# Two fused transformer blocks on one core: a 512-wide input product in the second block, a shorter inverse root, a one-step last stage, and a new interleaving

## The reference

```python
h = rmsnorm_2(x, g_pre) * (1.0 + scale[:, None, :]) + shift[:, None, :]
proj = jnp.einsum('bsd,de->bse', h, w_in)                # 1024 -> 3584
gu, gv, gg, rq, rk, rv, rg = jnp.split(proj, PROJ_SPLITS, axis=-1)   # 7 x 512
y_gmlp = gmlp_branch(gu, gv, gg, gmlp_ln_g, gmlp_ws, gmlp_bs)        # 4 groups of 128
y_ret = retention_branch(rq, rk, rv, rg, positions, ret_gn_g)        # 4 heads of 128
y = jnp.concatenate([y_gmlp, y_ret], axis=-1)
y = rmsnorm_2(jnp.einsum('bsm,md->bsd', y, w_out), g_post)
return x + gate[:, None, :] * y
```

## Time and profile before

| | |
|---|---|
| median of three executions | 3868.55 us |
| the profiled execution, its own time | 3869.71 us |
| its span, first to last instruction | 3867.9 us |
| TensorE busy | 3667.3 us, 95% |
| VectorE, ScalarE, GpSimd busy | 1910.7, 1698.8, 800.3 us |
| mean granted TensorE clock | 0.983 |
| TensorE idle in the waits listed, summed | 192.7 us |

### The profile page before, as it was taken

The page is one execution under the profiler, slowest core; times in us unless marked ns, Lnnn a source line. Parts: engine busy times, 40 slices in busy tenths (PEclk is TensorE's granted clock), DMA queues, the critical chain, the costliest instruction groups (busy, mean ns, idle before and its releaser), DMA issues.

```text
span 3867.9 us, 55010 instructions
## 1 busy us (share of the span) xinstructions
PE 3667.3 (95%) x21288; PEld 3203.9 (83%) x21288; DVE 1910.7 (49%) x4115; ACT 1698.8 (44%) x3455; POOL 800.3 (21%) x704
## 2 busy tenths in 40 slices
PE   7999889999998999999999999999999999999998
PEld 6888777888778888888878988888879987888897
DVE  4346563545656664546545555344567753111443
ACT  4334544555655444535544444343556543111322
POOL 3443333444454332110011100011000000000100
PEclk9999899999999999999999999999999999999999
DMA  6887557677676567455454556445453455545454
GB/s 167 270 252 208 176 166 254 217 254 267 238 251 223 182 228 275 162 192 177 158 187 145 170 193 218 166 170 188 155 201 132 145 191 209 195 175 199 170 185 145
DMA packets 327701, 760.01 MB, mean 196 GB/s; under 512 B 52625, under 2 KB 212369, under 8 KB 271122
## 3 DMA queue, kind: packets, MB, share of 16 engines
q1 hardware_dynamic: 266386, 720.83, 53.7%
q10 hardware_dynamic: 61056, 35.67, 3.5%
HBM read 581.00 MB, written 175.39 MB: 196 GB/s over the span
## 4 chain that ended last, share of the span: by engine, by line
PE 75%; DVE 12%; ACT 6%; issue 3%; ACTq 2%; POOL 1%; DMA 1%; SPq 0%; DVEq 0%
PE PS L1375 21%; PE PS L1377 21%; PE PS L1376 21%; PE PS L1493 2%; PE PS L1483 2%; PE PS L1474 2%; PE PS L1475 2%; PE PS L1507 1%; DVE PP L2093 1%; POOL WF L2322 1%; ACTq L1716 1%; PE PS L1453 1%; DVE BIG L1947 1%; ACT WF L1613 1%; DVE PT L2050 1%
## 5 line engine op out<-in xcount | busy, mean ns | idle before, releaser
L1375 PE MATMUL PS<-WF,BIG 128*128 128x256 f32 (+1 forms) x2328 | 726.7, 312 | 17.4 <-POOL WF L2322 6.5
L1377 PE MATMUL PS<-WF,BIG 128*128 128x256 f32 (+1 forms) x2328 | 712.4, 306 | 0.0
L1376 PE MATMUL PS<-WF,BIG 128*128 128x256 f32 (+1 forms) x2328 | 712.3, 306 | 0.0
L1375 PE MATMUL PS<-BIG,WF 128*128 128x512 f32 (+1 forms) x1792 | 687.1, 383 | 12.9 <-DVE BIG L1947 8.0
L1377 PE MATMUL PS<-BIG,WF 128*128 128x512 f32 (+1 forms) x1792 | 676.7, 378 | 0.0
L1376 PE MATMUL PS<-BIG,WF 128*128 128x512 f32 (+1 forms) x1792 | 676.3, 377 | 0.0
L2322 POOL TENSOR_TENSOR WF<-RAW,WF 128x512 fp32r<-128x512 f32 x380 | 507.0, 1358 | 746.7 <-ACT WF L1613 746.5
L1375 PEld LDWEIGHTS PS<-WF,BIG 128*128 128x128 f32 x2328 | 450.5, 194 | 44.1 <-issue 6.6
L1376 PEld LDWEIGHTS PS<-WF,BIG 128*128 128x128 f32 x2328 | 451.0, 194 | 21.3 <-issue 2.4
L1377 PEld LDWEIGHTS PS<-WF,BIG 128*128 128x128 f32 x2328 | 450.7, 194 | 18.1
L1375 PEld LDWEIGHTS PS<-BIG,WF 128*128 128x128 f32 x1792 | 342.9, 191 | 74.0 <-issue 12.1
(11 more groups left out here) (225 smaller groups left out, 6362.1 us busy)
## 6 DMA issues: line engine op xcount, KB each, us to landing
WF<-scratch_WS SPq DMA_DIRECT2D x264, 1024.0 KB, 5.0
scratch_WS<-WF SPq DMA_DIRECT2D x110, 1024.0 KB, 6.8
W<-scratch_WS SPq DMA_DIRECT2D x66, 1024.0 KB, 4.9
RAW<-in_w_in SPq DMA_DIRECT2D x84, 512.0 KB, 4.4
KV<-scratch_KS SPq DMA_DIRECT2D x60, 512.0 KB, 6.2
QQ<-scratch_QS SPq DMA_DIRECT2D x192, 128.0 KB, 4.6
XH<-in_x SPq DMA_DIRECT2D x32, 512.0 KB, 7.2
scratch_QS<-STG ACTq DMA_DIRECT2D x96, 128.0 KB, 3.8
```

What stands on the lines that cost most here:

```text
L1375: pe.matmul(o, Ah, Bh, start=first, stop=False)
L1376: pe.matmul(o, Ah, Bl, start=False, stop=False)
L1377: return pe.matmul(o, Al, Bh, start=False, stop=last)
```

## The change

1. **512 wide.** The first two blocks of the first four units of the second block's input product are laid out as one wide block (`wide("w_in_2", ...)`) and worked by `t_mixed` with `gemm_w`; `take_w` copies a bank of one token tile and 512 columns into the two buffers. The units' order becomes r0, r1, r2, g0, r3, g1. The gate block of g0 and all of r3 and g1 stay as they were. Both buffers of a unit are asked for together.
2. **Root in three VectorE steps.** The variance is kept as -0.5 v, Ln takes scale -2, and the Newton step's last two operations become one.
3. **Last stage.** ScalarE squares each half of a row from PSUM (`square_o`), VectorE multiplies the bank with the row of the gate while copying it out (`take_o`), the two sums of squares are added and the root taken (`rstd_out`), and `finish` is one operation (times root, plus x). In the last chunk the last two token tiles are worked one after the other (`apart`) and finished singly. `load_row` for the gate's row goes ahead of the `load_y` of the next chunk on the DMA queue.
4. **Start.** The first two `split_w` stand ahead of the first and the third of the four `turn_x`.
5. **Places.** `HALF_STEPS` is another table of the same length (1452) and sum (749).
6. A wait for a memset of the retention state is added to the first `rst` step of chunk 0.

```diff
-    return [units[i] for i in (2, 3, 0, 4, 5, 1)]
+    return [units[i] for i in (2, 3, 4, 0, 5, 1)]
+WIDE_UNITS = 4
...
-    r += [("w_in_2", "cols", q) for unit in mix_units() for q in unit[2]]
+    units = mix_units()
+    for n, (kind, i, req) in enumerate(units):
+        both = wide("w_in_2", req[0] + req[1]) if n < WIDE_UNITS else [("w_in_2", "cols", q) for q in req[0:2]]
+        r += both + [("w_in_2", "cols", q) for q in req[2:]]
...
-                for i, (v, j) in enumerate(((0, 0), (1, 0), (0, 1), (1, 1), (0, 2), (1, 2), (0, 3), (1, 3))):
+                for i in range(8):
+                    v, j = (i // 4, i % 4) if apart and g else (i % 2, i // 2)
...
+        def t_mixed(w, rd, done, ready=False):
+            for g in range(2):
+                if g and late:
+                    flush(0, (3,))
+                us = unit(), unit()
+                banks = [bank.take(done("frees", us[v])) for v in range(2)]
+                for i, (v, j) in enumerate(((0, 0), (0, 1), (1, 0), (1, 1), (0, 2), (0, 3), (1, 2), (1, 3))):
+                    u, (b, before) = us[v], banks[v]
+                    do(("gemm_w", u, w, 2 * g + v, j, b, before if j == 0 else (), rd))
+                    if g and v:
+                        released(w, j, ("mm", u) if j == 3 else ("quarter", u, j))
+                        split_half(True)
+                    if ready and not g and 3 < i < 7:
+                        flush(0, (i - 4,))
+                    if j == 3:
+                        done("do", u, b, 2 * g + v)
+                    yield 1.37
...
-        turn_round(("n1", 0), 0, scaled("n1", 0, 0), "n1", ())
+        split_half()
+        turn_round(("n1", 0), 0, scaled("n1", 0, 0), "n1", (), kps=(0, 1))
+        split_half()
+        turn_round(("n1", 0), 0, scaled("n1", 0, 0), "n1", (), kps=(2, 3))
...
+            do(("load_row", "gp", c, rows_free))
             if c < NC - 1:
                 yield "att", c + 1
                 for g in range(2):
                     load_y(c + 1, g)
-            do(("load_row", "gp", c, rows_free))
...
-                dve.tensor_scalar(t, t, -0.5, 1.5, ALU.mult, ALU.add).then_inc(*inc("norm_step", ("y3",) + key))
-                on.wait_ge("y3", *key)
-                dve.tensor_tensor(r, r, t, ALU.mult).then_inc(*inc("norm_step", ("rstd",) + key))
+                dve.scalar_tensor_tensor(r, t, 1.5, r, ALU.add, ALU.mult).then_inc(*inc("norm_step", ("rstd",) + key))
...
+            def square_o(c, u, b, t, i, after):
+                on.wait_ge("mm", u)
+                for e in after:
+                    on.wait_ge(*e)
+                act.activation(junk[:, 0:512], PS[b][:, :], ACT.Square,
+                               accum_out=SS[:, 4 * i + t:4 * i + t + 1]).then_inc(*inc("squared", ("sqo", c, t, i)))
...
+            def take_o(c, u, b, t, i, after):
+                ns = slice(512 * i, 512 * i + 512)
+                on.wait_ge("sqo", c, t, i)
+                on.wait_ge("row", "gp", c)
+                for e in after:
+                    on.wait_ge(*e)
+                dve.tensor_tensor(og[:, t, ns], PS[b][:, :], ROW[:, ns], ALU.mult).then_inc(*inc("o_taken", ("oc", u)))
...
+            def finish(c, t, key, made):
+                on.wait_ge("rstd", *key)
+                for e in made:
+                    on.wait_ge(*e)
+                dve.scalar_tensor_tensor(og[:, t, :], og[:, t, :], RSTD[:, t:t + 1], xh[:, t, :], ALU.mult,
+                                         ALU.add).then_inc(*inc("out_added", ("fz", c, t)))
```

More of the change, by code:

```diff
@@ L209 @@
 HALF_STEPS = (
[L210 to L219, removed]
@@ L854, in taken, with both_taken, done @@
                     return done
-                groups = [[0, 1]] + [[i] for i in range(2, len(req))] if not nun else [[i] for i in range(len(req))]
-                for blk in groups:
[L857 to L862, removed]
+                def both_taken():
+                    afters = []
+                    for i in range(2):
+                        buf = (pbn + i) % 4
+                        while pb_held[buf] is None:
+                            run()
+                        afters.append(pb_held[buf])
+                        pb_held[buf] = None
+                        bufs.append(buf)
+                        last.append([])
+                    def done(what, u, b=None, t=None):
+                        if what == "frees":
+                            return ("pc", u)
+                        do(("take_w", u, b, tuple(bufs[0:2]), t, afters[0] + afters[1]))
+                        for i in range(2):
+                            last[i].append(("pc", u))
+                    return done
+                groups = [[i] for i in range(len(req))] if nun >= WIDE_UNITS else [[0, 1]] + [[i] for i in range(2, len(req))]
+                for blk in groups:
+                    if len(blk) == 2:
+                        work = t_mixed(wide_weights(), rd, both_taken(), not nun)
+                    else:
+                        work = t_block([next_weights()], rd, [taken(blk[0])], None, (range(4), range(4, 8)))
+                    pbn += len(blk)
+                    for cost in work:
                         if small_first is None and count > 8:
@@ L887, in projections @@
                         yield cost
+                    if kind == "g" and len(blk) == 2:
+                        toks = [tuple(e) for e in last[0:2]]
+                        norms = [gmlp_norm(idx, i, bufs[i], toks[i]) for i in range(2)]
+                        mixes = [gmlp_mix(idx, i, bufs[i]) for i in range(2)]
+                        pending.extend([gap, norms[0], gap, gap, gap, norms[1], gap, gap, mixes[0], gap, gap, gap, mixes[1]])
+                        continue
                     for i in blk:
@@ L922, in done @@
                     g = tile // 2
-                    do(("take_o", c, u, b, tile, 512 * i, (("xp", y2, g, 3),)))
-                    if i:
-                        do(("square", "out", c, tile, "o", "junk", tile, (("oc", u),)))
-                    if i and tile % 2:
[L927 to L934, removed]
+                    do(("square_o", c, u, b, tile, i, last_square))
+                    last_square = (("sqo", c, tile, i),)
+                    do(("take_o", c, u, b, tile, i, (("xp", y2, g, 3),)))
+                    taken_o[tile, i] = ("oc", u)
+                    if i and c == NC - 1 and g:
+                        finish_tiles(g, [tile])
+                    elif i and tile % 2:
+                        finish_tiles(g, [tile - 1, tile])
+                    if i and tile % 2:
                         big_free[g] = (("mm", u),)
@@ L938, in projections @@
             ahead = (lambda kps: turn_round(("y", c + 1), 0, (("y", c + 1, 0),), "y", big_free[0], None, 2, kps)) if c < NC - 1 else None
-            yield from t_wide(wide_weights(), rd, out_taken(1), ahead)
-            rows_free = (("fy", c, 3),)
+            yield from t_wide(wide_weights(), rd, out_taken(1), ahead, False, c == NC - 1)
+            rows_free = (("oc", mm["n"] - 2), ("oc", mm["n"] - 1))
             pace[0] = 1.0
-            gb_free = tuple(("out", c, t) for t in range(4)) + (("sq", "out", c, 3),)
+            gb_free = tuple(("out", c, t) for t in range(4)) + last_square
     def attention():
```

102 lines of the change are left out of this document (73 added, 29 removed).

## The result

The changed kernel took 3770.5 us in the median of four executions (3765.1 to 3779.7), against 3869.3 us before: a ratio of 0.9746, 95% interval 0.9725 to 0.9768, 99 us less. The forecast was 3841 with a range of 3828 to 3857. The sign was right and the size was not: the change brought 70 us more than forecast.

What follows compares the result with a forecast made beforehand. TensorE, busy 95% of the span, was taken as the bound. Terms -20.1 + 4 - 2.5 - 1 - 4.3 - 4 = -27.9 from the profiled 3869.7 gave 3841.8, said as 3841 after a median correction; range 3828 to 3857.

Steps and rivals of the forecast that it cites:

- Places: New table of attention half steps, same sum and nearly the same course: -4 us, ends -12 and +8, the least known term.
- knot argument: Places 120 to 129: entries 7, 10 and 3 in a row thinned to at most 6; that stretch can give some 5 us.
- 0 +/- 2: Second block's input product: weight cover holds, and units' order, both buffers at once and memset's wait move nothing TensorE waits for.
- Wide matmuls: Second block's input product: 1536 pairs of 256-wide matmuls become 512-wide, 13.1 ns less each, 20.1 us in all, 5.0 per chunk.
- Bank waits: Wide blocks: a bank is wanted again after 2.7 us in place of 5.8, late ScalarE copies cost +4 us, ends 0 and +14.
- Start: First chunk: TensorE's first product at 14.8 in place of 18.07, 3.3 us earlier; taken as -2.5, ends 0 and -3.3.
- End: Behind the last matmul: 7.5 us to the span's end in place of 11.8, -4.3 us, ends -3.5 and -5.0.
- Root: Norm chains: one VectorE operation of 0.17 and a gap of 0.03 less in each; -1 us, ends 0 and -2.
- Half hidden: Rival, chance 0.17: beside attention freed time only lengthens TensorE's waits, 10 of the 20.1 us stay: 3855.
- slower: Rival, chance 0.05: ScalarE's copies miss the 2.7 us at nearly every tile and TensorE's clock falls in the pauses: 3880.
- equal overhead: Rival, chance 0.03: the wide matmul is no better per column than the pair, all 20.1 us missing: 3861.
- The places do better: Rival, chance 0.07: TensorE's waits in the first 600 us shrink by more than the knot, up to 12 us: 3831 or less.

Runs made afterwards that it cites:

- thin_knot: The kernel before with only table places 120 to 129 changed, same 26 half steps, at most 4 in a place: 3866.8 us (0.9989).
- no_w: The changed kernel with the narrow blocks and the old order of units, new table kept: 3812.8 us (0.9853 of the kernel before).
- no_p: The changed kernel with the old table of places: 3880.3 us (1.0028 of the kernel before).
- w_only: The kernel before with the wide blocks and the new order of units alone, old table: 3903.2 us (1.0087).
- start_only: The kernel before with the first two splits ahead of the turns, alone, old table: 3867.5 us (0.9990).

## Why the prediction was wrong, and where it was right

- **Places: the step that failed.** I compared the two tables by their sums, running sums and knots, found them alike, and put -4 with ends of -12 and +8. (The running sums differ by up to 15, not 13.) Measured: -39 on the old code, -110 on the new, where 47 us came outside the four input products and 65 inside. The knot argument itself held (thin_knot, -4.3). But each half step has to stand beside a certain product step, and sums can't see that. One place aside costs 104 to 115 us, one half step over one stage 30.
- **Changed code under an old fit.** I charged the wide blocks' new positions and the order "0 +/- 2". On the old table order alone costs 20 us and both 33. Without its new table the change would have been a loss of 11 us. A rival "the rest without a fitting table is slower" was not among mine.
- **Wide matmuls: right in size.** Last chunk, without attention: 188.8 for 192.9 us, 4.1 of the 5.0 forecast; no_w, with the same small edits, took 194.2 there, which gives 5.4. The spacing in the input product after the change, 72 starts in 16.32 us or 226.7 ns:

```profile
3543.39 0.39 PE L1444 MATMUL PS<-W,BIG 128*128 128x512 f32 x1
...
3559.71 0.39 PE L1444 MATMUL PS<-WF,BIG 128*128 128x512 f32 x1
```

  By the Trainium skill's overhead of about 2.5 ns a matmul (TensorE: Matmul & The Clock Gate, "Wait — 56ns, not 53.3ns?") this chunk would have gained 1.0 us, an estimate from 384 pairs. This trace does not agree: 226.7 ns is 13.4 above 512 columns at 2.4 GHz, as in the rows. In chunks 0 and 2 with the new table (no_w to after) the gain is 10.1 and 16.5 us where the matmuls account for 5.0 each; most of the rest is idle time of TensorE, which fell by 8.1 and 9.1 us.
- **Bank waits: right only with the old table.** I charged 4 us (to 14) for copies later than 2.1 us, counted in a trace with the old table. With that table the waits are there, 5.2 us in no_p and 5.6 in w_only. With the new one no product waits for `take_w`, though ScalarE idled until TensorE before only 31 of the 64 copies (us and times):

```profile
  PE PS L1444: 107.3, 31
```

  And most of what the wide form loses on the old table I had not priced at all: waits of attention and mixing.
- **Start: right in kind, a little small.** The first product starts at 14.25 where 14.8 was forecast, 3.8 us earlier and not 3.3. The edit alone is worth 3 to 4 us (0.4 to 7 by its interval) where -2.5 with an end of -3.3 stood. **End: right**, 7.3 us for 7.5.
- **Root: mis-sized.** -7 (3 to 10 by its interval) for -1. I counted only waits that name the scale behind a root. Those fell by 1.4 us (14.3 to 12.9 in six), near the forecast, but all waits of TensorE together fell by 8.3 (186.6 to 178.3). VectorE has 88 operations fewer (4115 to 4027) and is busy 17.7 us less. Whether the rest of the 7 us comes from shorter chains behind other waits or from the shift against the table is not shown.
- **Half hidden, slower, equal overhead:** none of these rivals came. "The places do better" had the right direction at chance 0.07, for a thinner knot; its 12 us were a third of the smallest worth measured.

Open: why a certain half step beside a certain product step costs what it costs was not taken apart. I showed the waits that grow, not a rule to foresee them. How the new table was found is not on record. How much of the wide blocks' 42 us on the new table is due to them and how much to a table that suits them can't be told, since no table made for the narrow blocks with the other edits was there to run.

## What to carry to other kernels

In a kernel that weaves two streams of work by a written-out table into strictly ordered queues, the table is part of the code's timing. An edit that changes a duration, an order or a count should be judged with the table laid anew; judged on the old one an edit that saves matmul time can show as a loss, as the wide blocks did here. And a forecast for such a change needs wide bounds for the table: here -39 to -110 us, 1 to 3% of the time, with sums that are the same.

Compare stages by a count of work that both traces share, not by time. A stage whose code is hardly touched and whose time falls points at the interleaving at once. And when two parts of a change depend on each other, split the crossed runs by stage: here the dependence sits in the rebuilt stages alone.

## What the runs showed that I had not expected

This is about the clock at the start. Before, TensorE's product matmuls ran at the lower level (1.2 GHz) from 18.07 until about 22.5, after a pause of 3.3 us. Their duration then falls:

```profile
22.27 0.41 PE L1376 MATMUL PS<-BIG,WF 128*128 128x256 f32 x1
...
22.64 0.27 PE L1375 MATMUL PS<-BIG,WF 128*128 128x256 f32 x1
```

After the change, with the products right behind the transposes, matmuls were at 0.28 us from 15.03. In start_only, which has this edit alone, they were from the second on:

```profile
14.29 0.28 PE L1497 MATMUL PS<-BIG,WF 128*128 128x256 f32 x1
```

So in this pair some clock was gained beside the 3.8 us by which the first product came earlier. An estimate: the 21 starts from 18.07 to 22.64 took 4.57 us where 119.9 ns each would be 2.5, and the three from 14.25 to 15.03 took 0.8 for 0.4, so 1.6 us. The stage fell by 4.9.

The pause is not the whole cause. In the traces of the eleven kernels with the new start, 1 to 10 product matmuls pass before they run at 0.28 us. In seven of the eight without it, 20 to 25 do, but in thin_knot, which has the same pause, one does.
